# Expert products regrouped by width, and the scaled second-key hits moved from VectorE to ScalarE

## The reference, cut to what matters

```python
q = jnp.einsum('bsd,dq->bsq', h, w_q).reshape(b, s_len, PEER_HEADS, 2, PEER_HALF)
scores = jnp.einsum('bshpc,hpnc->bshpn', q, sub_keys)          # 8 heads, 2 halves, 128 keys
top_s, top_i = lax.top_k(scores, PEER_TOPK)                     # 16 of each half
...
best_s, best_pos = lax.top_k(cand_s, PEER_TOPK)                 # 16 pairs of keys per head
gate = jax.nn.softmax(best_s, axis=-1)
...
u = jnp.take(expert_u, ib, axis=0)                              # expert = first_key * 128 + second_key
act = jax.nn.gelu(jnp.einsum('td,tkd->tk', xb, u), approximate=False)
vv = jnp.take(expert_v, ib, axis=0)
return jnp.einsum('tk,tkd->td', gb * act, vv)
```

## Time and profile before

| | |
|---|---|
| median of the three runs | 1297.62 us |
| lowest and highest of them | 1295.9 and 1298.31 us |
| the profiled execution, from its first to its last instruction | 1296.0 us |
| TensorE, VectorE, ScalarE, GpSimd busy in it | 99%, 76%, 50%, 8% |

### The profile page before, as it was taken

The page is one execution under the profiler, slowest core; times in us unless marked ns, Lnnn a source line. Parts: engine busy times, 40 slices in busy tenths (PEclk is TensorE's granted clock), DMA queues, the critical chain, the costliest instruction groups (busy, mean ns, idle before and its releaser), DMA issues.

```text
span 1296.0 us, 17206 instructions
## 1 busy us (share of the span) xinstructions
PE 1284.0 (99%) x7048; PEld 1089.6 (84%) x7048; DVE 986.4 (76%) x1265; ACT 650.7 (50%) x624; POOL 105.9 (8%) x142
## 2 busy tenths in 40 slices
PE   9999999999999999999999999999999999999998
PEld 6888878888789888988888888888888888888887
DVE  7557779889876875699989899997576666666663
ACT  6555563344455455464555565565454444444441
POOL 0101200000020000000000011011120000000000
PEclk9999999999999999999999999999999999999999
DMA  9515379996453134556777779998998787887860
GB/s 378 202 60 195 128 301 418 381 377 221 162 212 131 65 140 185 165 192 228 237 237 226 238 240 300 295 301 291 339 358 329 288 290 290 291 292 290 291 228 33
DMA packets 113726, 318.30 MB, mean 246 GB/s; under 512 B 7280, under 2 KB 74096, under 8 KB 92016
## 3 DMA queue, kind: packets, MB, share of 16 engines
q1 hardware_dynamic: 94944, 247.98, 53.8%
q0 software_dynamic: 18416, 68.17, 14.7%
q10 hardware_dynamic: 288, 1.05, 0.2%
HBM read 282.56 MB, written 34.61 MB: 245 GB/s over the span
## 4 chain that ended last, share of the span: by engine, by line
PE 89%; DVE 6%; ACT 2%; DMA 1%; issue 1%; POOL 0%; SPq 0%; DVEq 0%; ACTq 0%
PE psum L519 87%; PE psum L522 2%; DVE slab_lo L1687 2%; DMA hidden_store<-arena 1%; ACT arena L1379 1%; DMA slab_raw<-in_w_in 0%; ACT slab_hi L1246 0%; DVE arena L1982 0%; ACT arena L1287 0%; DVE arena L2243 0%; ACT arena L1249 0%; ACT arena L1269 0%; DVE arena L1946 0%; DVE residual L2432 0%; POOL statistics L466 0%
## 5 line engine op out<-in xcount | busy, mean ns | idle before, releaser
L1687 DVE TENSOR_TENSOR slab_lo<-slab_raw,slab_hi 128x2048 fp32r<-128x2048 f32 x206 | 469.4, 2287 | 176.4 <-ACT slab_hi L1246 176.4
L1246 ACT ACTIVATE slab_hi<-slab_raw 128x2048 fp32r<-128x2048 f32 x206 | 392.7, 1912 | 232.2 <-PE psum L519 226.7
L519 PE MATMUL psum<-slab_hi,x_parts 128*128 128x512 f32 x1520 | 480.8, 392 | 2.5 <-ACT x_parts L1293 0.9
L519 PE MATMUL psum<-x_parts,slab_hi 128*128 128x512 f32 (+1 forms) x1344 | 420.3, 371 | 1.1 <-DVE arena L2229 1.1
L519 PEld LDWEIGHTS psum<-slab_hi,x_parts 128*128 128x128 f32 x1520 | 285.4, 188 | 65.2 <-issue 5.6
L519 PE MATMUL psum<-x_parts,slab_lo 128*128 128x256 f32 x1184 | 330.9, 279 | 0.0
L519 PE MATMUL psum<-slab_lo,x_parts 128*128 128x512 f32 x760 | 295.9, 389 | 0.0
L519 PEld LDWEIGHTS psum<-x_parts,slab_hi 128*128 128x128 f32 x1344 | 241.8, 188 | 46.3 <-DVE arena L2229 1.7
L519 PEld LDWEIGHTS psum<-x_parts,slab_lo 128*128 128x128 f32 x1184 | 223.6, 189 | 0.0
L519 PEld LDWEIGHTS psum<-slab_lo,x_parts 128*128 128x128 f32 x760 | 142.8, 188 | 28.8 <-issue 0.2
L519 PE MATMUL psum<-slab_hi,weighted_hi 128*128 128x512 f32 x296 | 116.0, 392 | 0.1
(11 more groups left out here) (276 smaller groups left out, 1049.5 us busy)
## 6 DMA issues: line engine op xcount, KB each, us to landing
slab_raw<-in_ex_u SPq DMA_DIRECT2D x128, 512.0 KB, 5.5
slab_raw<-in_ex_v SPq DMA_DIRECT2D x64, 1024.0 KB, 6.4
arena<-in_w_ada SPq DMA_DIRECT2D x24, 1024.0 KB, 7.1
slab_raw<-in_w_gu SPq DMA_DIRECT2D x22, 1024.0 KB, 7.1
slab_raw<-in_w_in SPq DMA_DIRECT2D x21, 1024.0 KB, 8.7
hidden_store<-arena POOLq DMA_DIRECT2D x32, 512.0 KB, 5.6
arena<-hidden_store POOLq DMA_DIRECT2D x32, 512.0 KB, 5.3
arena<-gates_store POOLq DMA_DIRECT2D x32, 512.0 KB, 6.6
```

Source lines behind the costliest of these rows:

```text
L519: return PE.matmul(out, lhsT, rhs, start=start, stop=stop)
L1246: ACTE.activation(slab_hi[:, slot, :], raw[:, slot, :], ACT.Copy).then_inc(hi_made[slot], 1)
L1687: DVE.tensor_tensor(slab_lo[:, slot, :], raw[:, slot, :], slab_hi[:, slot, :].bitcast(f32), ALU.subtract).then_inc(lo_made[slot], 1)
```

## The change

Two edits, independent of each other. In `expert_half` the 8 products of 512 columns of a tile are issued ahead of its 8 products of 256 columns, and the wait for `slab_lo` moves behind the first tile's 512-column products. In the gate steps, `small_hit_b` is made by ScalarE (function `small_hits`, a copy with a scale) where VectorE made it; VectorE signals `second_hits_made` after `hit_b`, ScalarE waits for that and signals `small_hits_made`, and TensorE's gate step waits for it beside `gated_hits_made`. In ScalarE's order, `small_hits` stands behind `hi(S_EU + s + 4)` of the half and ahead of `copy_gates`, for the gate steps of the same half.

```diff
@@ names of shared semaphores
-    "attention_exp_made": (("fox_exp_made", 16), ("mem_exp_made", 8)),
+    "attention_exp_made": (("fox_exp_made", 16), ("mem_exp_made", 8), ("small_hits_made", NSTEP)),
...
-    "choice_made": (("gate_softmax_made", 1), ("first_keys_made", 1), ("second_keys_made", 1)),
+    "choice_made": (("gate_softmax_made", 1), ("first_keys_made", 1), ("second_keys_made", 1), ("second_hits_made", NSTEP)),
@@ TensorE, gate_step
                 PE.wait_ge(*after("gated_hits_made", i + 1))
+                PE.wait_ge(*after("small_hits_made", i + 1))
@@ TensorE, expert_half
-                take(n)
-                bh, bl = parts(n % NSLOT, KT, S)
+                slot = n % NSLOT
+                PE.wait_ge(hi_made[slot], n // NSLOT + 1)
+                bh, bl = parts(slot, KT, S)
                 for m in range(2):
                     col = slice(m * P, m * P + P)
                     for k in range(KT):
                         mm(ps[:, bank + m, :], bh[:, k, col], xx[:, :, k, :], k == 0, False)
+                    if m == 0:
+                        PE.wait_ge(lo_made[slot], n // NSLOT + 1)
+                    for k in range(KT):
                         ins = mm(ps[:, bank + m, 0:S], bl[:, k, col], xh[:, k, :], False, k == KT - 1)
@@ ScalarE
+            def small_hits(i):
+                n = i % 2
+                ACTE.wait_ge(*after("second_hits_made", i + 1))
+                ACTE.activation(small_hit_b[n], hit_b[n], ACT.Copy, scale=1.0 / REST_UP).then_inc(sem("small_hits_made"), 1)
...
+                for i in range(gates_due(s - 1), gates_due(s)):
+                    small_hits(i)
                 for i in range(gates_due(s - 1), gates_due(s)):
                     copy_gates(i)
@@ VectorE, gate_step
-                V(DVE.tensor_tensor(hit_b[n], each_row, of_token(key_b), ALU.is_equal))
+                DVE.tensor_tensor(hit_b[n], each_row, of_token(key_b), ALU.is_equal).then_inc(sem("second_hits_made"), 1)
...
-                DVE.tensor_scalar(small_hit_b[n], hit_b[n], 1.0 / REST_UP, None, ALU.mult)
```

## The result

The changed kernel took 1438.54 us (median of 4 runs, 1432.41 to 1438.90) against 1296.80 us for the kernel before on the same chips (4 runs): a ratio of 1.108, interval 1.106 to 1.109. It is slower by 142 us. The forecast was 1402 us with a range of 1390 to 1432: the direction and the place were right, and a quarter of the loss (36.5 of 141.7 us) was missed. The profiled execution has a span of 1431.1 us, 135.1 us over that of before, and is the fastest of the four by 6 us.

A forecast was written before the change was run, and what follows sets the result against it. The prediction took TensorE, busy 99% of the span, as the bound. 1296.0 + 99.8 (stalls) - 2.5 (product order) + 7 (clock) = 1400.3 us, with 1.6 us to the median 1402 us; range 1390 to 1432 us.

The forecast's parts named there:

- TensorE is the bound, and every wait on it is paid in full: Whole kernel: TensorE is busy 99% of the span and 89% of the chain, so any added wait lengthens the time.
- Place and size of the stalls: In the 24 halves with gate steps, the gate step starts 3.67 us (even) or 4.62 us (odd) later; 99.8 us in all.
- the faster float16 copy of a rival: ScalarE's scaled copy takes 0.42 us, stalls are 15 us less and no clock fall comes: 1380 us, chance 0.08.
- Nothing stacks on the stall: Behind TensorE's new wait, ScalarE, VectorE and slab loads are ready in time, so no second wait is added.
- VectorE's relief is worth nothing: VectorE loses 32 scalings, 13.5 us at most, none on the chain, so this gains nothing by itself.
- The order of the products, 2.5 us of gain: Grouped 512- and 256-column products run at 347 ns a pair throughout, where alternating ones take 347 or 354 ns.
- The clock, 7 us: TensorE's clock falls to 1.2 GHz in four of the twelve odd holes, at 1.9 us each.
- one of the forecast's own signs of being wrong: In the halves with gate steps, the forecast would be wrong if the even holes too took the clock down.
- My bound of 46 us for all 24 holes: Upper bound of the clock's cost on TensorE, with a fall in all 24 holes; the lower bound was none.
- the clock falls in nearly every odd hole, and in some even ones: Rival for TensorE's holes: twelve falls cost 23 us (1418 us), all 24 give 1441 us; chance 0.2 for over 1412 us.
- The 1.6 us between the profiled span and the median: Kernel before: the profiled execution is 1.6 us under the median of the runs, added to 1400.3 us for 1402 us.

The follow-up runs named there:

- filled to fit: Changed kernel with 8 (even halves) or 10 (odd halves) idle matmuls in TensorE's hole before the gate step; 1394.83 us against 1296.22 us before.
- the run with the early copies: Changed kernel with ScalarE making the scaled hits at the end of the round one half before; 1296.28 us against 1296.52 us for the kernel before.
- the early copies in alternating order: Changed kernel with scaled hits made one half earlier and products in the alternating order of before; 1297.26 us against 1297.80 us before.
- the 512 numbers in one piece: Kernel before with only the new product order, 512-column products reading two neighbouring parts of x (wrong values); 1296.77 us against 1297.80 us before.
- a later run: Changed kernel with the scaled copy ahead of `hi` in ScalarE's round, still behind its wait for the half; 1367.36 us against 1296.22 us before.
- the odd ones filled: Changed kernel with idle matmuls only in the holes after odd halves, those after even halves left open; 1417.38 us against 1296.22 us before.
- the even holes filled: Changed kernel with idle matmuls only in the holes after even halves, those after odd halves left open; 1417.60 us against 1296.22 us before.

## Why the prediction was wrong, point by point

- *TensorE is the bound, and every wait on it is paid in full*: right. Idle time, slower work and nothing else make up the 135 us of the profiled span, all of it between 733.6 and 1033.6 us.
- *Place and size of the stalls*: right. Forecast 3.51 and 4.46 us of idle time in even and odd halves, found 3.52 and 4.46; forecast 99.8 us in all, found 98.6 with the clock held up (and the hand-over 2 us shorter). The scaled copy takes 1.045 us (1.04 forecast), and the faster float16 copy of a rival doesn't exist. The Trainium skill, page "ScalarE: Activation LUTs", section "What ACT_TABLE_LOAD costs", gives one speed for float32 and bfloat16, an estimated 1.04 us for this copy. It doesn't name float16; this trace agrees for float16 too, with 1.045 us.
- *Nothing stacks on the stall*: right, by the runs in which it was shortened or moved away and the one in which it was filled to fit.
- *VectorE's relief is worth nothing*: right, though it was smaller than forecast (busy time down by 9 us in the 24 halves of the run with the early copies, not 13.5).
- *The order of the products, 2.5 us of gain*: the mechanism, two paces in the alternating order, was there, and the size was off. The grouped pair costs 349 ns, not the 347 I took from streams of one width, and that difference eats the gain: ratio 1.0003 where the forecast of 2.5 us asks for 0.998.
- *The clock, 7 us*: this is the term that failed. Its step was "One fall at such a price in four of the twelve odd holes is 7 us". Measured: about 41 us in the medians, and 39 us in the profiled execution, which had 19 falls of an estimated 1.3 to 3.0 us each (half of TensorE's work in each low stretch), 2.1 us on average. So the price of 1.9 us was about right, and the count was not. The price was read from lengths, against the rule that distances between starts say what a matmul costs; by starts the first six matmuls give 5.85 - 1.45 = 4.40 us where six idle matmuls of 512 columns in the filled holes take 0.43 us each, 1.8 us less in all:

```profile
1.45 4.56 PE L519 MATMUL psum<-hidden 128*128 128x512 f32 x6 [1.45 <-DVE hidden L1812]
5.85 1.04 PE L522 MATMUL psum<-ident,residual 128*128 128x128 f32 x8
```

For the count I read the end of the program, where the clock stayed up for 3.6 us after the last matmul, as the shortest idle time that takes it down. It was one sample of something that varies, and the same end shows it in other runs: 2.9 us with the early copies in alternating order, whose last matmul ends at 1291.93 us (rows below), and 4.4 us with the 512 numbers in one piece (1290.75 to 1295.12 us). In the changed kernel the first fall came 2.0 us into a hole, and in a later run falls followed holes of 2.7 us.

```profile
1291.93:1294.70 2.77, 0.00 (x0) 0.00 (x0) 1.43 (x3) 0.00 (x0) 0.00 (x0) 1.00 0.55 209
1294.80:1295.80 1.00, 0.00 (x0) 0.00 (x0) 0.00 (x0) 0.00 (x0) 0.00 (x0) 0.50 0.15 55
```

In the changed kernel all 12 odd holes and 7 of the 12 even ones had a fall, and with the odd ones filled all 12 even ones had, which was one of the forecast's own signs of being wrong. My bound of 46 us for all 24 holes did hold, in part by luck, since fewer falls came at a higher price each; the range stopped short of it. The rival "the clock falls in nearly every odd hole, and in some even ones" is what happened, at its upper end.
- *The 1.6 us between the profiled span and the median*: nearly right for another reason. A span is shorter than the time of its own run, by 1.3 us in the changed kernel (1431.1 against 1432.41).

The Trainium skill, page "TensorE: Matmul & The Clock Gate", section "HAM oscillation — how this bites in real kernels", tells of pauses between bursts that take the clock down over and over. The trace agrees, with a mean clock of 0.85 over 300 us, and I gave that too small a chance.

Still open: why the alternating order runs at either of two paces and stays there for whole stretches, and why a 512-column product costs 230 ns in the grouped order. I can't say either which start of a hole brings a fall within it and which brings one later.

## What to carry to other kernels

A step moved to an idle engine costs what stands ahead of it in that engine's order, not what it takes by itself: a copy of 1.04 us cost 4.1 us each half here because it stood behind work that the consumer itself releases, and nothing at all one half earlier. Where the waiting engine is TensorE and holes recur like those of 2.7 to 4.5 us here, add the clock: some 41 us on top of 99, which idle matmuls of the right length in the holes took back. A bound for the clock from a single idle time is no bound; take all holes as falls for the range's upper end.

## What the runs showed of the hardware

- The clock fell to 1.2 GHz as early as 2.0 us after TensorE had gone idle in the changed kernel (1.9 us with the even holes filled), and in other holes only once work had begun again; holes of 3.5 and of 4.5 us brought it down equally often (12 times of 12 each, if they alone were open), holes of 2.67 us 8 times of 12, holes of 1.2 us (24) and 1.7 us (12) never.
- A fall costs about half of the time that TensorE works in the low stretch (79 us of work at the low clock, 39 us more busy time): by that estimate, in the changed kernel, 1.3 to 1.7 us where it lasts 3.4 us, 2.4 to 3.0 us where it lasts 6.8 us, 2.1 us on average. Both lengths follow holes of both kinds.
- The pair of a 512- and a 256-column product costs 347 or 354 ns in turn and 349 ns in runs of eight of a kind.
- VectorE can be busy 97% of a stretch and still have nothing to give: 9 us less busy time there changed the time by nothing that a measurement to 0.1% can tell.
- TensorE's hand-over from ScalarE took 0.14 to 0.15 us when it sat idle and 0.06 us when idle matmuls had kept it at work (24 holes each).
